# Reciprocal square roots of twelve norms: reciprocal on VectorE and square root on ScalarE in place of logarithm and exponential on ScalarE

## What is computed

```python
def rms_norm(x, gain):
    xf = x.astype(jnp.float32)
    y = xf * lax.rsqrt(jnp.mean(xf * xf, axis=-1, keepdims=True) + EPS)
    return (y * gain.astype(jnp.float32)).astype(x.dtype)

def layer_norm(x, g, b):
    xf = x.astype(jnp.float32)
    mu = jnp.mean(xf, axis=-1, keepdims=True)
    var = jnp.mean(jnp.square(xf - mu), axis=-1, keepdims=True)
    return ((xf - mu) * lax.rsqrt(var + LN_EPS) * g + b).astype(x.dtype)

# hybrid_layer, twice
    h = rms_norm(x, attn_pre_gain)                      # n1
    ...
    x = x + rms_norm(mixed @ w_out, attn_post_gain)     # n2
    h = rms_norm(x, ffn_pre_gain)                       # n3
    x = x + rms_norm(conv_ffn(h, ...), ffn_post_gain)   # n4

# second_block, layer 0 and layer 1
        h = layer_norm(ALPHA * h + mix, ...)            # l0, l1
        ffn = hierarchical_moe(h, ...)                  # 32 experts, the best 2 of one group
        h = layer_norm(ALPHA * h + ffn, ...)            # m0, m1
```

## Time and profile before

| | us |
|---|---|
| median of 3 runs | 4267.36 |
| lowest and highest run | 4262.03, 4273.49 |
| the profiled execution's own time | 4275.79 |
| its span, first to last instruction | 4274.0 |
| mean granted clock of TensorE | 0.897 of full speed |
| busy: PE, VectorE, ScalarE | 3638.4, 2476.5, 1937.9 |

### The profile page before, as it was taken

The page is one execution under the profiler, slowest core; times in us unless marked ns, Lnnn a source line. Parts: engine busy times, 40 slices in busy tenths (PEclk is TensorE's granted clock), DMA queues, the critical chain, the costliest instruction groups (busy, mean ns, idle before and its releaser), DMA issues.

```text
span 4274.0 us, 55643 instructions
## 1 busy us (share of the span) xinstructions
PE 3638.4 (85%) x16820; PEld 2852.2 (67%) x16820; DVE 2476.5 (58%) x3756; ACT 1937.9 (45%) x3108; POOL 207.3 (5%) x253
## 2 busy tenths in 40 slices
PE   7987889997987789998987777599999696749996
PEld 5854668785764558876766665488888474538884
DVE  3257646633247646643555553599999426448995
ACT  3235443323235533333332222388888224427883
POOL 0000000000000000000000000111111000011110
PEclk9967899998977899998988888799999798869998
DMA  3210112222220012222210000699999220039994
GB/s 135 94 50 0 45 64 93 93 89 80 93 79 0 20 60 94 97 85 88 90 59 0 0 0 3 234 358 368 363 366 387 87 89 5 0 138 348 383 382 163
DMA packets 161960, 553.72 MB, mean 130 GB/s; under 512 B 28800, under 2 KB 28864, under 8 KB 160576
## 3 DMA queue, kind: packets, MB, share of 16 engines
q1 hardware_dynamic: 141760, 518.70, 33.7%
q0 software_dynamic: 16832, 16.90, 1.2%
q10 hardware_dynamic: 3264, 16.78, 1.0%
HBM read 555.40 MB, written 38.85 MB: 139 GB/s over the span
## 4 chain that ended last, share of the span: by engine, by line
PE 78%; DVE 11%; issue 5%; ACT 3%; DMA 1%; POOL 0%; ACTq 0%; DVEq 0%; POOLq 0%; SPq 0%
PE psum L611 20%; PE psum L613 20%; PE psum L612 20%; PE psum L646 3%; PE psum L826 2%; PE psum L708 2%; PE psum L720 1%; PE psum L738 1%; DVE arena L1715 1%; PE psum L676 1%; PE psum L939 1%; DVE arena L1878 1%; PE psum L1028 1%; PE psum L909 1%; DVE arena L1591 1%
## 5 line engine op out<-in xcount | busy, mean ns | idle before, releaser
L2143 DVE TENSOR_TENSOR ew_r<-arena,ehigh_r 128x1024 fp32r<-128x1024 f32 x648 | 749.4, 1219 | 13.8 <-ACT ehigh_r L1427 13.8
L1569 DVE TENSOR_TENSOR ring_rounded<-ring,highs 128x1024 fp32r<-128x1024 f32 x302 | 368.8, 1223 | 665.5 <-ACT highs L1093 665.5
L611 PE MATMUL psum<-oab_r,highs 128*128 128x512 f32 x1520 | 607.5, 400 | 50.2 <-DVE h_r L1584 17.5
L1427 ACT ACTIVATE ehigh_r<-arena 128x1024 fp32r<-128x1024 f32 x648 | 630.6, 1052 | 0.0
L613 PE MATMUL psum<-oab_r,ring_rounded 128*128 128x512 f32 x1520 | 597.2, 393 | 0.0
L612 PE MATMUL psum<-h_r,highs 128*128 128x512 f32 x1296 | 508.5, 392 | 0.0
L1093 ACT ACTIVATE highs<-ring 128x1024 fp32r<-128x1024 f32 x302 | 318.7, 1057 | 351.7 <-PE psum L613 324.7
L611 PEld LDWEIGHTS psum<-oab_r,highs 128*128 128x128 f32 x1520 | 288.2, 190 | 122.2 <-DVE h_r L1584 38.3
L611 PE MATMUL psum<-ehigh_r,xT_high_r 128*128 128x512 f32 x864 | 352.4, 408 | 13.9 <-DVE ew_r L2143 7.6
L613 PE MATMUL psum<-ehigh_r,xT_low_r 128*128 128x512 f32 x864 | 341.7, 396 | 0.0
L612 PE MATMUL psum<-ew_r,xT_high_r 128*128 128x512 f32 x864 | 338.6, 392 | 0.0
(11 more groups left out here) (350 smaller groups left out, 6357.8 us busy)
## 6 DMA issues: line engine op xcount, KB each, us to landing
arena<-in_moe_w SPq DMA_DIRECT2D x648, 512.0 KB, 6.0
ring<-in_wstream SPq DMA_DIRECT2D x328, 512.0 KB, 3.3
rows_in_m<-arena ACTq DMA_DIRECT2D x4, 2048.0 KB, 9.0
arena<-rows_out_m ACTq DMA_DIRECT2D x8, 1024.0 KB, 5.6
x<-in_xT SPq DMA_DIRECT2D x1, 2048.0 KB, 11.7
result<-x SPq DMA_DIRECT2D x1, 2048.0 KB, 6.3
const<-in_const SPq DMA_DIRECT2D x1, 1004.0 KB, 4.9
arena<-rows_in_m,arena POOLq DMA_INDIRECT x58, 6.9
```

Of the source, the lines that this page charges most:

```text
L611: pe.matmul(acc, lhs[0], rhs[0], start=start, stop=False)
L1427: act.activation(ehigh_r[p], ew[:, p, :], ACT.Copy).then_inc(expert_cast[mi], 1)
L1569: dve.tensor_tensor(ring_r[:, c % R, :], ring[:, c % R, :], highs[:, c % HIGHS, :].bitcast(F32), ALU.subtract).then_inc(weights_split, seq ...
L2143: TT(ew_r[p], ew[:, p, :], ehigh_r[p].bitcast(F32), ALU.subtract).then_inc(expert_split[mi], 1)
```

## The change

`rstd` and the two activations of `layer_norm` on ScalarE go. In their place VectorE takes the sum from PSUM, divides by 1024 and adds the epsilon (a TENSOR_SCALAR over 128x512), then takes the reciprocal (RECIPROCAL over 128x512, in place); ScalarE waits for that and takes the square root, in place; VectorE waits for the root and scales as before. The set that holds the square root is loaded by an explicit instruction while the sums are made: after the squares in n1 and in the layer norms, ahead of the eight output tiles for n2 (n3 keeps the same set), and at the start of the down projection for n4.

```diff
+ROOTS = "sqrt_and_others"
...
-            def rstd(stage, div=D, eps="eps", bank=7):
-
-                act.wait_ge(pe_done, seq.at(f"{stage}.ss"))
-                act.activation(rs, psum[:, bank, :], ACT.Ln, bias=cc(eps), scale=1.0 / div) \
-                    .then_inc(act_done, seq.step())
-                act.wait_ge(act_done, seq.so_far())
-                act.activation(rs, rs, ACT.Exp, scale=-0.5).then_inc(act_done, seq.step(f"{stage}.rs"))
+            def root(stage, dst):
+
+                act.wait_ge(dve_done, seq.at(f"{stage}.inv"))
+                act.activation(dst, dst, ACT.Sqrt).then_inc(act_done, seq.step(f"{stage}.rs"))
...
                 squares("n1", x)
+                act.preload_act_table_set(ROOTS)
                 cast_weights()
                 cast_weights()
-                rstd("n1")
+                root("n1", rs)
...
                     high("mix", r, sigb_r, h)
+                act.preload_act_table_set(ROOTS)
                 for r in range(8):
...
-                rstd("n2")
+                root("n2", rs)
...
-                rstd("n3")
+                root("n3", rs)
...
                     high_g(k)
+                act.preload_act_table_set(ROOTS)
                 for k in range(PAIRS):
...
-                rstd("n4")
+                root("n4", rs)
...
-                act.wait_ge(pe_done, seq.at(f"{stage}.ss"))
-                act.activation(rs_, psum[:, 6, :], ACT.Ln, bias=cc("lneps"), scale=1.0 / D) \
-                    .then_inc(act_done, seq.step())
-                act.wait_ge(act_done, seq.so_far())
-                act.activation(rs_, rs_, ACT.Exp, scale=-0.5).then_inc(act_done, seq.step(f"{stage}.rs"))
+                act.preload_act_table_set(ROOTS)
+                root(stage, rs_)
...
+            def inverse(stage, dst, bank=7, eps=EPS):
+
+                dve.wait_ge(pe_done, seq.at(f"{stage}.ss"))
+                dve.tensor_scalar(dst, psum[:, bank, :], 1.0 / D, eps, ALU.mult, ALU.add).then_inc(dve_done, seq.step())
+                dve.wait_ge(dve_done, seq.so_far())
+                dve.reciprocal(dst, dst).then_inc(dve_done, seq.step(f"{stage}.inv"))
+
             def scaled(stage, dst, src, gain):
 
+                inverse(stage, rs)
                 dve.wait_ge(act_done, seq.at(f"{stage}.rs"))
...
+                inverse(stage, rs_, 6, LN_EPS)
                 dve.wait_ge(act_done, seq.at(f"{stage}.rs"))
```

## The result

| | us |
|---|---|
| changed kernel, median of 6 runs | 4297.78 (4281.42 to 4300.74) |
| kernel before, median of 6 runs | 4269.2 (4262.03 to 4273.49) |
| ratio | 1.0063, 95% interval 1.0045 to 1.0080 |
| predicted | 4296.2, range 4283 to 4310 |

The change makes the kernel 28.6 us slower by the medians, 19 to 34 us by the interval of the ratio; 28.8 had been predicted. The profiled execution of the changed kernel took 4298.53 us, with a span of 4296.4.

The account below looks back on a forecast made before the run. PE was taken to bound the kernel, with 78% of the last-ending chain. Twelve norms at +2.09 us (+25.1) and uncovered loads (+3.7) make +28.8 on 4267.36: 4296.2 us, range 4283 to 4310.

Parts of the forecast that it names:

- What is on the path: In each of twelve norms, sum's arrival to first scaled tile is serial: 2.66 us before, 4.75 predicted, +25.1 in all.
- The price of RECIPROCAL: VectorE's reciprocal over 128x512 in each norm: 6 ns per element, read as six cycles, so 3.35 us.
- The rival of an ordinary rate: Reciprocal in each norm costs about 0.61 us, like an addition; kernel at 4263.3 us, no difference; chance 0.10.
- the one of eight cycles per element: Reciprocal in each norm takes 4.4 us at 8.3 ns per element; +41 us, kernel at 4308; chance 0.08.
- The other terms: Rest of each norm's new chain: TENSOR_SCALAR from PSUM 0.68 us, square root 0.63, three hand-overs 0.09 together.
- The loads: Three new uncovered table loads: +1.28 us in each of two routings, +1.1 ahead of the second attention; +3.7 together.
- the term of 2.6 us: Uncovered loads before the small exponentials of the routings after l0 and l1: 2 x 1.28 us.
- The switch that costs more than its load: Rival: each switch of table set costs a further 1.35 us; +16.7 us, kernel at 4284; chance 0.02.
- The clock: Rival: longer pauses lengthen PE's 1.2 GHz stretches after 11 norms, 19 us more, kernel at 4315; chance 0.05.
- The explicit loads: Preloads of the root's set in n1, n2, n4 and layer norms are covered; uncovered they would cost 1.28 us each.

Follow-up runs that it names:

- the three loads alone: Kernel before, with the root's set loaded after each layer norm's exponential, so the routings and second attention must reload theirs; norms unchanged: 4274.51 us, ratio 1.0012.
- with all: Kernel before, with the joint logarithm-exponential set loaded in the twelve norms, ahead of and in the delta rule's loop, and in the second attention's norm: 4244.2 us.

## Why the prediction was right

- **What is on the path.** That everything from the sum to the first scaled tile is serial, and nothing hides in it, was the first step. Three times the reciprocal gave 80.3 us of 81, and PE's pause grew behind every norm.
- **The price of RECIPROCAL.** It was taken from a difference of 12 ns between two small sizes: 3.35 us predicted, 3.353 measured. The step of 12 ns alone left 2.7 to 3.5 us open; that the forecast was met to 3 ns comes from reading 6 ns per element as six whole cycles, and measured are 6.25. That reading was a guess that came true. The rival of an ordinary rate (0.61 us) and the one of eight cycles per element (4.4 us) fall with it. The repeat count of 8 that the Trainium skill names ("VectorE: DVE Perf Modes", section "First, the fixed hardware budget") is not the rate here.
- **The other terms.** TENSOR_SCALAR from PSUM 0.68 predicted, 0.691 measured; the root 0.63 and 0.629; hand-overs 0.09, and 4.78 - 0.69 - 3.35 - 0.63 = 0.11. A norm: 4.75 predicted, 4.78 measured.
- **The loads.** Two at 1.28 as predicted. That of the second attention was put at 1.1; PE's pause grew from 4.80 to 6.07, 1.27, since the copies came to be what PE waits for. VectorE's wait in the routing was to go up from 6.10 to 7.4 and went to 6.5 and 6.2. The load is there in full, but PE's 32 transposes, which ScalarE evicts ahead of its exponential, ran faster. After l0, before and after the change:

```profile
2662.69 6.17 PE L917 MATMUL psum<-const,x 128*128 128x128 f32 x32
```

```profile
2682.03 5.14 PE L918 MATMUL psum<-const,x 128*128 128x128 f32 x32
```

Over these stretches the granted clock was 0.58 before and 0.71 after. From the transposes' start to the exponential's are 7.94 us before and 8.30 after, 0.4 more and not 1.28, and 0.4 more after l1 too: the term of 2.6 us came to 0.7. This is not the luck of one execution: in the six profiles of kernels with a reciprocal the transposes took 4.9 to 5.4 us in 11 of 12 stretches, in the four with logarithm and exponential 5.9 to 6.5 in 7 of 8. What raises the clock earlier there was not tested. In the kernel with the three loads alone the transposes after l0 took 6.2 as before, and the wait was 7.4 at the longest.

- **The switch that costs more than its load** (the drain of 1380 ns of the Trainium skill, "ScalarE: Activation LUTs", section "What ACT_TABLE_LOAD costs") is ruled out for the new loads too: the activation starts 0.01 to 0.02 us after the load.
- **The clock.** No extra price of the longer pauses showed. In the two routings PE ran faster and gave back nearly 2 us, where the prediction had "shifts of a microsecond or two of either sign". As a source of scatter it was underrated: by the local terms the two profiled executions should differ by 25.4 + 2.6 + 1.3 = 29.3 us, and their spans differ by 22.4. PE was busy 8.4 us less in the second (3638.4 and 3630.0 us) with the same 16820 matmuls; beyond the two routings it wasn't followed where. A single pair of executions would not have been enough.
- **Luck.** That the medians met the forecast to 0.2 us is luck: the interval runs from 19 to 34 us, and the second comparison of the same two kernels gave 31.9 us by the medians. Shown are the terms, not the last microseconds of their sum.
- **The explicit loads.** The prediction said that they have cover and would cost 1.28 us each without it. They have it; but in the kernel without them the compiler's loads have it too, which the prediction didn't consider.

## What to carry to other kernels

Where two activations follow each other on the path, look first at what stands between them: here 1.28 of 2.66 us was a table load that one explicit load of a common set ahead removes. By the medians this gave 16 us with the loads in the twelve norms and 24 with all, while moving half of the work to another engine cost 29. A reciprocal over 128x512 on VectorE took 3.35 us, five to six times a plain pass (0.61 to 0.69); two small sizes in a trace hinted at that rate before anything was built. And a set of functions is state: whoever replaces it changes what the next user pays, however far on in the program that is. Here it was 1.28 us more for each of three exponentials in one case, and 2.7 us less at the second attention in the other.

## What the runs showed of the hardware that was not expected

The compression stage (256 matmuls of 128x62 in two layers, L676 before, L677 after) runs at one of two speeds, and which one changes from execution to execution. In the changed kernel's first profile and in its second, groups of PE in the stage of the first layer:

```profile
L677 PE MATMUL psum<-arena,ring 128*128 128x62 f32 x128 | 26.4, 409 | 2.3 <-ACT arena L1152 2.3
```

```profile
L677 PE MATMUL psum<-arena,ring 128*128 128x62 f32 x128 | 14.5, 275 | 2.3 <-ACT arena L1152 2.3
```

The code is the same, the stage takes 26.4 us in one and 14.5 in the other, and the spans were 4296.4 and 4285.0. Over the stage of the first layer (length, PE, weight loads, VectorE, ScalarE and GpSimd busy, granted clock, DMA share, GB/s), again in the first and in the second profile:

```profile
226.10:252.50 26.40, 26.35 (x128) 26.23 (x128) 5.49 (x5) 1.60 (x2) 0.00 (x0) 0.53 0.43 146
```

```profile
225.30:239.80 14.50, 14.46 (x128) 14.32 (x128) 5.53 (x5) 1.52 (x3) 0.00 (x0) 1.00 0.71 228
```

So where the stage takes 26.4 us it runs nearly throughout at the lower level, 1.2 GHz, though PE is busy all the time, and where it takes 14.5 us at 2.4. In the 25 us ahead of it the granted clock was 1.00 in both, and PE had then stood still for the same 2.3 us. In the ten profiles of this study (the kernel before, the changed kernel twice, and seven others), each with two such stages, a stage took 14.5 us 3 times in 20 and 25.0 to 27.6 us the other times. What decides it is open. It was not tried to force either level. One such stage is worth 12 us, as large as nearly half of what was to be measured. The lowest run of several kernels here lies 12 to 19 us below its median (4281.42 against 4297.78 for the changed kernel, 4283.75 against 4302.49 without explicit loads). The three profiles with a stage at the higher level are each of the lowest run of their kernel in its group: 4283.75 and 4288.19 without explicit loads, 4287.05 (median 4299.95) for the changed kernel. For the lowest runs without a profile it is only likely.
